# Splitting weights on ScalarE and VectorE instead of GpSimd in a hybrid decoder step

## What is computed

```python
xn = rmsnorm(x, norm1_g)
rg_x, rg_y, q, k, v, g_lr, g_out, m_a, m_b = split(xn @ w_in)
xc = causal_conv4(rg_x);  h = rglru(xc, ...)           # gated linear recurrence over time
ya = (h * gelu(rg_y)) @ w_branch_a
o  = gla(q * dk**-0.5, k, v, log_alpha)                # chunked gated linear attention, state S
yb = (rmsnorm(o) * g * silu(g_out)) @ w_branch_b
x  = x + (sigmoid(m_a) * ya + sigmoid(m_b) * yb) @ w_out
u  = causal_conv3(rmsnorm(x, norm2_g) @ w_ffn_up);  gate, val = split(u)
x  = x + (gelu(gate) * val) @ w_ffn_down
y  = rmsnorm(x, final_norm_g)                          # also all final states
```

## Time and profile before

| | us |
|---|---|
| three timed runs, median | 1968.67 (1965.29 to 1969.84) |
| the profiled execution, device time | 1968.59 |
| its span in the trace | 1966.8 |
| TensorE matmul busy | 1914.4 (97%) |
| VectorE busy | 906.0 (46%) |
| GpSimd busy | 701.9 (36%) |
| ScalarE busy | 420.9 (21%) |

### The profile page before, as it was taken

The page is one execution under the profiler, slowest core; times in us unless marked ns, Lnnn a source line. Parts: engine busy times, 40 slices in busy tenths (PEclk is TensorE's granted clock), DMA queues, the critical chain, the costliest instruction groups (busy, mean ns, idle before and its releaser), DMA issues.

```text
span 1966.8 us, 29051 instructions
## 1 busy us (share of the span) xinstructions
PE 1914.4 (97%) x11890; PEld 1885.9 (96%) x11890; DVE 906.0 (46%) x916; ACT 420.9 (21%) x480; POOL 701.9 (36%) x324
## 2 busy tenths in 40 slices
PE   7999999999999999999999999999999999999997
PEld 6999888888889999999999999999999999999997
DVE  5211277787865311141134555536253535354546
ACT  4000144555532100020011121102010101010115
POOL 3333232232234343344344333333333333334353
PEclk9999998999999999999999999999999999999999
DMA  5221123222212111131113211111111111111112
GB/s 192 87 89 43 44 88 109 89 77 91 77 43 75 43 43 53 43 130 48 48 48 125 65 44 43 44 54 44 44 44 53 43 44 45 53 43 44 53 52 86
DMA packets 48167, 127.11 MB, mean 65 GB/s; under 512 B 6952, under 2 KB 20008, under 8 KB 48080
## 3 DMA queue, kind: packets, MB, share of 16 engines
q1 hardware_dynamic: 27744, 88.39, 13.5%
q10 hardware_dynamic: 20352, 37.64, 5.5%
HBM read 108.14 MB, written 18.14 MB: 64 GB/s over the span
## 4 chain that ended last, share of the span: by engine, by line
PE 92%; DVE 4%; issue 3%; ACT 1%; DMA 0%; DVEq 0%; SPq 0%
PE acc L416 84%; PE acc L594 1%; PE acc L755 1%; PE small L514 1%; PE small L517 1%; DVE rg_xc_h L1327 1%; PE small L526 1%; DVE rg_xc_h L1324 1%; DVE rg_ext L1149 0%; PE small L607 0%; DVE gla_bc_keT L1214 0%; PE small L755 0%; PE small L489 0%; DMA x_in<-in_x 0%; PE small L533 0%
## 5 line engine op out<-in xcount | busy, mean ns | idle before, releaser
L382 POOL TENSOR_TENSOR w_hi<-w_raw,ones 128x1024 fp32r<-128x1024 f32 x149 | 288.3, 1935 | 1215.5 <-PE acc L416 1203.7
L416 PE MATMUL acc<-xn_hi,w_hi 128*128 128x346 f32 (+1 forms) x2520 | 553.8, 328 | 15.9 <-DVE xn_lo L1136 12.1
L416 PE MATMUL acc<-xn_lo,w_hi 128*128 128x346 f32 (+1 forms) x2520 | 541.8, 323 | 0.0
L416 PE MATMUL acc<-xn_hi,w_lo 128*128 128x346 f32 (+1 forms) x2520 | 540.1, 323 | 0.0
L416 PEld LDWEIGHTS acc<-xn_hi,w_hi 128*128 128x128 f32 x2520 | 427.5, 190 | 21.5 <-issue 12.9
L416 PEld LDWEIGHTS acc<-xn_lo,w_hi 128*128 128x128 f32 x2520 | 429.7, 190 | 0.0
L416 PEld LDWEIGHTS acc<-xn_hi,w_lo 128*128 128x128 f32 x2520 | 428.6, 190 | 0.0
L384 POOL TENSOR_TENSOR w_lo<-w_raw,w_hi 128x1024 fp32r<-128x1024 f32 x149 | 384.2, 2578 | 11.7
L1520 DVE TENSOR_TENSOR residual<-acc,residual 128x1032 f32<-128x1032 f32 x56 | 69.0, 1232 | 115.8 <-PE acc L416 115.8
L1491 DVE SCALAR_TENSOR_TENSOR tmp<-val_ext,ffn_params,tmp 128x1024 f32<-128x1024 f32 x48 | 97.9, 2040 | 39.4 <-ACT tmp L1069 36.6
L1491 DVE SCALAR_TENSOR_TENSOR gate_conv<-gate_ext,ffn_params,gate_conv 128x1024 f32<-128x1024 f32 x48 | 92.0, 1917 | 40.6 <-ACT gate_conv L1063 37.7
(11 more groups left out here) (216 smaller groups left out, 2082.6 us busy)
## 6 DMA issues: line engine op xcount, KB each, us to landing
w_raw<-in_w SPq DMA_DIRECT2D x153, 512.0 KB, 3.5
ha_scratch<-rg_gelu_ha ACTq DMA_DIRECT2D x8, 519.0 KB, 3.5
h<-ha_scratch ACTq DMA_DIRECT2D x8, 519.0 KB, 7.0
residual<-in_x ACTq DMA_DIRECT2D x8, 519.0 KB, 7.6
gla_qk_pair<-qk_scratch ACTq DMA_DIRECT2D x8, 512.0 KB, 5.8
smp_v_rows<-smp_v_scratch ACTq DMA_DIRECT2D x8, 512.0 KB, 6.5
out_gla_sample<-smp_state ACTq DMA_DIRECT2D x8, 512.0 KB, 3.8
smp_state<-in_gla_state ACTq DMA_DIRECT2D x7, 512.0 KB, 5.0
```

The costliest lines, as they stand in the source:

```text
L382: nc.gpsimd.tensor_tensor(whi[s], raw[s], one, ALU.mult).then_inc(w_hi_done[s], 1)
L416: mm = nc.tensor.matmul(acc[g][:, n, 0:cw], w[s][:, t * P:(t + 1) * P], x[:, c0 + n * cw:c0 + (n + 1) * cw], start=a, stop=z)
```

## The change

The loop of splits on GpSimd is removed; it keeps the units 1 and 2 and the last three, so 147 of the 153 units move. A new function `w_high` on ScalarE makes the hi part with a Copy, and `w_low` on VectorE subtracts it from the raw weight. Calls of both stand at fixed places of the two streams, one pair for each unit u, behind the eviction of unit u, and split unit u+2.

```diff
             split(0, 1)
-            with pool.Fori(1, (N_UNITS - GRP) // 2) as i:
-                split(i, 0)
-                split(i, 1)
+            split(1, 0)
...
+            def w_high(u, per=0, i=0):
+                s, n = slot_of(u), nth(u, per, i)
+                act.wait_ge(w_loaded[s], 16 * n + 16)
+                act.wait_ge(unit_done[s], n)
+                nc.scalar.activation(whi[s], raw[s], ACT.Copy).then_inc(w_hi_done[s], 1)
...
                 nc.scalar.activation(gy[:, late], gy[:, late], ACT.Gelu_apprx_tanh).then_inc(gelu_ready, 1)
+                w_high(U_RG + 3, 2, j)
                 plain()
                 act.wait_ge(gate_mm, 2 * j + 1)
...
+            def w_low(u, per=0, i=0):
+                s, n = slot_of(u), nth(u, per, i)
+                dve.wait_ge(w_hi_done[s], n + 1)
+                nc.vector.tensor_tensor(wlo[s], raw[s], whi[s].bitcast(F32), ALU.subtract).then_inc(w_split[s], 1)
...
                 nc.vector.tensor_copy(col(rgo, j, RGW, RGW), ext[:, C + 3 - RGW:C + 3]).then_inc(rgo_kept, 1)
+                w_low(U_RG + 2, 2, j)
                 o_copy(n, PAIR, c0, 0, sb6)
...
                 state(n, PAIR, 1, sb7)
+                w_low(U_RG + 3, 2, j)
...
                     evacuate(U_GO + s, 2, i, g, T[s][:, late], cols=LATE)
+                    w_low(U_GO + 2 + s, 2, i)
...
                 nc.vector.tensor_tensor(view3(e_t[:, 2 + L0:2 + L1]), accl[g], view3(rms[:, late]), ALU.mult).then_inc(acc_free[g], 1)
+                w_low(u + 2, per, i)
                 dve.wait_ge(bias_sem, F + 1)
...
                 nc.vector.tensor_tensor(view3(blkd(X2, m)), accd[g], view3(blkd(X2, m)), ALU.add).then_inc(acc_free[g], 1)
+                v = (2, 5, 7).index(m) if m in (2, 5, 7) else GRP
+                if v < n_low:
+                    w_low(u_last - GRP + 3 + v, per, i)
```

More of the change, by code:

```diff
@@ L813, in _ @@
                 for s, g in ((0, 1), (1, 0)):
+                    w_high(U_QKV + s + 2, 2, i)
                     act.wait_ge(acc_free[g], G_QKV[g] + i + 1)
@@ L889, in sample_tokens @@
                 nc.scalar.activation(t, bank[0:NS, :], ACT.Copy).then_inc(sT_ready, 1)
+            w_high(U_QKV + 10)
             ke_tokens(0, NMETA)
@@ L894, in _ @@
             load_qk(PAIR, NMETA)
+            w_high(U_QKV + 11)
+            with act.Fori(1, 4) as i:
+                w_high(U_QKV + 10, 2, i)
+                w_high(U_QKV + 11, 2, i)
             act.wait_ge(acc_free[0], G_RG[0])
@@ L958, in rg_body @@
                     .then_inc(xbias_ready, 1)
+                w_high(U_RG + 2, 2, j)
                 act.wait_ge(sS_ready, j + 1)
@@ L1008, in gate_o @@
                     nc.scalar.activation(T[s][:, late], T[s][:, late], ACT.Silu).then_inc(silu_done, 1)
+                    w_high(U_GO + 2 + s, 2, i)
                     plain()
@@ L1016, in _, with gate_b @@
                 gate_o(i)
-            with act.Fori(0, KB) as j:
+            def gate_b(j):
                 act.wait_ge(acc_free[1], G_B[1] + j + 1)
                 nc.scalar.activation(T[2][:, late], T[2][:, late], ACT.Tanh, scale=0.5).then_inc(tanh_done, 1)
+                w_high(U_B + 2, 2, j)
+            with act.Fori(0, KB - 1) as j:
+                gate_b(j)
+                w_high(U_B + 3, 2, j)
+            gate_b(KB - 1)
             for k in range(KB):
@@ L1027, in _ @@
                 act.dma_start(blkl(HA, k), ha_scr[k][:, late]).then_inc(hl_loaded[k], 16)
+            w_high(U_B + 3, 2, KB - 1)
             for k in range(KB):
@@ L1030, in _, with gate_a @@
                 nc.scalar.activation(blkl(HAH, k), blkl(HA, k), ACT.Copy).then_inc(hah_done, 1)
-            with act.Fori(0, KB) as j:
+            def gate_a(j):
                 act.wait_ge(acc_free[1], G_A[1] + j + 1)
                 nc.scalar.activation(T[2][:, late], T[2][:, late], ACT.Tanh, scale=0.5).then_inc(tanh_done, 1)
+                w_high(U_A + 2, 2, j)
+            with act.Fori(0, KB - 1) as j:
+                gate_a(j)
+                w_high(U_A + 3, 2, j)
+            gate_a(KB - 1)
             act.wait_ge(acc_free[1], G_OUT[1])
@@ L1038, in _ @@
                 if k == KB - 1:
-                    ready(U_OUT - 1)
+                    w_high(U_A + 3, 2, KB - 1)
                     for m in range(KB):
@@ L1045, in _ @@
             for k in range(KB):
+                w_high(U_OUT + k + 2)
                 act.wait_ge(acc_free[1 - k % 2], G_OUT[1 - k % 2] + k // 2 + 1)
@@ L1055, in _, with ffn_block @@
             norm_factor(sum2_mm, lnr2_done, r2_done, LATE)
-            def ffn_block(F, grp):
+            def ffn_block(F, grp, u, per, i):
                 plain()
@@ L1064, in ffn_block @@
                                      bias=fpr[:, bass.ds(3 * UB + F, 1)]).then_inc(gbias_ready, 1)
+                w_high(u + 2, per, i)
                 act.wait_ge(gconv_step, 3 * F + 3)
@@ L1070, in ffn_block @@
                                      bias=fpr[:, bass.ds(3 * UB + FB + F, 1)]).then_inc(vbias_ready, 1)
+                w_high(u + 3, per, i)
                 act.wait_ge(act_done, F + 1)
@@ L1076, in _, with ffn_group, down_high @@
             GU, GD = GRP, KB // 2
-            def ffn_group(F0_, grp, half):
+            NU, ND = 2 * GRP, GRP
+            per = 2 * (NU + ND)
+            def ffn_group(F0_, grp, half, u0, i=0):
                 for f in range(GRP):
-                    ffn_block(F0_ + f, grp + f)
+                    ffn_block(F0_ + f, grp + f, u0 + 2 * f, per, i)
                     ffn_hi(half, f)
+            def down_high(u0, i, n):
+                for v in range(n):
+                    w_high(u0 + NU + v + 2, per, i)
             act.wait_ge(set_f, 4)
-            ffn_group(0, 0, 0)
+            ffn_group(0, 0, 0, U_FFN)
             gper = 2 * (GU + GD)
             with act.Fori(0, NGRP // 2 - 1) as i:
-                ffn_group(2 * GRP * i + GRP, GU + gper * i, 1)
+                ffn_group(2 * GRP * i + GRP, GU + gper * i, 1, U_FFN + NU, i)
+                down_high(U_FFN + NU, i, ND)
                 act.wait_ge(acc_free[0], G_FFN[0] + 2 * GU + GD + gper * i)
-                ffn_group(2 * GRP * i + 2 * GRP, 2 * GU + GD + gper * i, 0)
+                ffn_group(2 * GRP * i + 2 * GRP, 2 * GU + GD + gper * i, 0, U_FFN + 2 * NU + ND, i)
+                down_high(U_FFN + 2 * NU + ND, i, ND)
                 act.wait_ge(acc_free[0], G_FFN[0] + 3 * GU + 2 * GD + gper * i)
             n = NGRP // 2 - 1
-            ffn_group(GRP * (NGRP - 1), GU + gper * n, 1)
+            ffn_group(GRP * (NGRP - 1), GU + gper * n, 1, U_FFN + NU + n * per)
+            down_high(U_FFN + NU + n * per, 0, 1)
             act.preload_act_table_set(LN_EXP)
@@ L1161, in stage_qk @@
                     evacuate(U_QKV + s, 2, i, g, (rt, it)[s])
+                    w_low(U_QKV + s + 2, 2, i)
             stage_qk(0)
@@ L1279, in _ @@
             evacuate(U_QKV + 8, 0, 0, 1, blk(V, 0))
+            w_low(U_QKV + 10)
             scores(0, NMETA)
             evacuate(U_QKV + 9, 0, 0, 0, blk(V, 1))
+            w_low(U_QKV + 11)
             with dve.Fori(1, 4) as i:
                 evacuate(U_QKV + 8, 2, i, 1, blk(V, 2 * i))
+                w_low(U_QKV + 10, 2, i)
                 evacuate(U_QKV + 9, 2, i, 0, blk(V, 2 * i + 1))
+                w_low(U_QKV + 11, 2, i)
             o_copy(0, NMETA, 0, 0, sb7)
@@ L1414, in _ @@
                 evacuate(U_B, 2, j, 1, T[2][:, late], cols=LATE)
+                w_low(U_B + 2, 2, j)
                 dve.wait_ge(tanh_done, j + 1)
@@ L1418, in _ @@
                     .then_inc(acc_free[0], 1)
+                w_low(U_B + 3, 2, j)
             for k in range(KB):
@@ L1430, in merge_gate @@
                 evacuate(U_A, 2, j, 1, T[2][:, late], cols=LATE)
+                w_low(U_A + 2, 2, j)
             def merge(j):
@@ L1509, in ffn_block, with add @@
                 nc.vector.tensor_tensor(blkd(AL, b), act_t[:, down_c], blkd(AH, b).bitcast(F32), ALU.subtract).then_inc(actl_done, 1)
-            def add(n_down, grp, m, u_last, per, i):
+            def add(n_down, grp, m, u_last, per, i, n_low):
                 g = 1 - m % 2
@@ L1524, in _, with ffn_group @@
             per, gper = 2 * (NU + ND), 2 * (GU + GD)
-            def ffn_group(F0_, u0, grp0, half, n_down=None, i=0):
+            def ffn_group(F0_, u0, grp0, half, n_down=None, i=0, n_low=GRP):
                 def down(m):
-                    add(n_down, grp0 + GRP, m, u0 + NU + ND - 1, per, i)
+                    add(n_down, grp0 + GRP, m, u0 + NU + ND - 1, per, i, n_low)
                 for f in range(GRP):
```

4 lines of the change are left out of this document (3 added, 1 removed).

## The result

The changed kernel takes 1937.68 us (median of 4 runs, 1936.29 to 1939.25) against 1968.46 us for the kernel before (4 runs): a ratio of 0.9846, 95% interval 0.9829 to 0.9863. The forecast was 1939 us. The profiled execution takes 1936.35 us, its span 1934.5, which is 32.3 us less than the span before.

The account below looks back on a forecast made before the run. TensorE, busy 97% of the span, bounds the kernel; its waits in the recurrent rounds were the gain. 1968.6 - 35.2 (rounds) + 4.9 (down products) + 0.2 (output gate) = 1938.5, so 1939 us; range 1930 to 1955.

Parts of the forecast that it names:

- The cause: Recurrent rounds: GpSimd's split holds VectorE's 10-column product and sum, so TensorE waits 3.0 us for scores before `O_pair`.
- The hold: Recurrent rounds: time GpSimd's split adds to VectorE's 10-column product and sum, 1.57 + 2.08 = 3.65 us a round.
- The Copy on the path: Recurrent rounds: a weight Copy on ScalarE before the first tanh adds 0.8 us to the path to the scores.
- the wait: Recurrent rounds: TensorE's wait before `O_pair` shrinks from 3.0 to about 0.1 us, and the half clock should go.
- the bound without residue: Recurrent rounds: upper bound on the saving, 5.3 us a round, 37 in all.
- The 0.2 us for `o_copy`: Recurrent rounds: a subtraction ahead of `o_copy` delays the state product that needs it; 0.2 us a round added.
- VectorE's subtraction at the round's end: Recurrent rounds: the added subtraction behind the gelu is covered by VectorE's slack; costed at nothing, at most 1 us a round.
- The down products: FFN groups' last blocks: `add(0)` ends late for TensorE's column block 2, 0.7 us each, 4.9 us for seven.
- The output gate's first unit: Output gate: the split of U_GO + 2 comes 0.2 us late for TensorE, once.
- Short operations that are long by themselves: Rival, recurrent rounds: the 10-column operations are long without GpSimd, nothing is freed; 1982.6 us, chance 0.09.
- Half the hold: Rival, recurrent rounds: only the 10-column product is freed, wait 2.2 us, clock still drops; 1968 us, chance 0.05.
- Leftover wait: Rival, recurrent rounds: added Copy and subtraction run late, 1 to 2 us more a round; 1946 to 1960 us, chance 0.15.

Follow-up runs that it names:

- e2: Kernel before, all splits still on GpSimd, only the split of each recurrent round's first unit waits for `rgo_kept`; 1932.72 us, ratio 0.9823.
- e3: Kernel before, only the second half (`w_lo`) of the split of each round's first unit waits for `rgo_kept`; 1940.73 us, ratio 0.9867.
- e1: Kernel before, only the splits of the recurrent rounds (units 19 to 34) moved to ScalarE and VectorE; 1933.04 us, ratio 0.9827.
- e4: Changed kernel, the split of each recurrent round's first unit back on GpSimd at its old time; 1976.52 us, ratio 1.0034.
- e5: Changed kernel, in each FFN group's last block the value unit's subtraction put behind `add(0)`; 1934.85 us, ratio 0.9834.
- e7: Changed kernel, the splits of the recurrent rounds (units 19 to 34) back on GpSimd; 1972.72 us, ratio 1.0017.
- e6: Changed kernel, the Copy ahead of each recurrent round's first tanh cut into 16 Copies of 64 columns; 1944.71 us, ratio 0.9883.

## Why the prediction was right, step by step

**The cause** was right. The hold was estimated at 3.65 us a round; 4.09 us for the two operations became 0.31, so 3.78 us were freed. e2 and e3 show that it is the overlap in time, and that each half of the split holds the operation beside it. The order in the kernel before becomes plain with one more of its rows, between those of the earlier trace rows:

```profile
417.28 2.31 DVE L1325 TENSOR_TENSOR_SCAN rg_xc_h<-rg_a,rg_i_b 128x1040 f32<-128x1040 f32 x1
```

`w_hi` runs first and the product waits for it; the scan is then ahead of `w_lo` (417.28 against 417.41), which lasts 4.38 us there and 2.38 in e2: it waited for the scan. The sum then waits for `w_lo`. The engines pass one thing to and fro, and VectorE lost its turn twice.

The Trainium skill's page SBUF — State Buffer, section Who interferes with whom, says just this: the two exclude each other for the whole instruction, in order of issue. The traces agree, with 0.14 us and 2.30 us for the same operation in one execution (e1). The Trainium skill's page Perfetto Trace Analysis, section GPSIMD Engine Instruction, calls GpSimd's spans unreliable, which I gave as the word against it; here the ends that match within 0.03 us were real, since moving GpSimd's instruction moved VectorE's end (e2, e3).

**The Copy on the path** was put at 0.8 us and is 0.2; this is the term of the sum that was most off. The gate product of this round, by the timelines of the kernel before and of the changed one:

```profile
394.94 1.93 PE L594 MATMUL acc<-rg_xc_h,rg_gate_weights 128*128 128x350 f32 x6
```

```profile
379.26 1.93 PE L592 MATMUL acc<-rg_xc_h,rg_gate_weights 128*128 128x350 f32 x6
```

The prediction counted from 395.10, where the chain takes this product up, 0.16 us late; its sum is not hurt, as it ends a round on the same kind of row, but before and after must be counted from one kind of start. From the gate product to the scores' end a round took 425.07 - 394.94 = 30.13 us and now takes 405.80 - 379.26 = 26.54, which is 3.59 less, of the 3.78 that were freed: 0.19 is left for the Copy. ScalarE's first tanh does start 0.54 us later (2.60 behind the gate product against 2.06), but at the 10-column product 0.17 is left (20.80 against 20.63). e2, which frees the same without a Copy, ends its scores 26.37 us behind the gate product (408.51 - 382.14), 0.17 less, and e4 agrees with 0.2. I carried a delay at its source to the end of the chain as if nothing on the way had slack.

**So the wait** of 0.1 us became a margin of 0.47, and a round is TensorE's own work alone: 38.05 us, against the 26.96 + 11.03 = 37.99 that the prediction had for it and 38.35 that it forecast. Seven rounds gave 37.28, the bound without residue (37), not 35.2. The 0.2 us for `o_copy` went the same way.

**VectorE's subtraction at the round's end** was costed at nothing, rightly: VectorE still idles 2.64 us ahead of the operation that had 2.72 in the earlier trace rows. What covers its 1.23 us, by the timelines, is the sample state's first operation, L1298, which took 3.24 us beside GpSimd's split in this round and takes 1.14 now; the prediction named it without a number.

**The down products** were put at 0.7 us each, 4.9 in all; the stretch grew by 3.6, 0.5 each: column block 2 starts 8.65 us behind the group's first `act_lo` product where it was 8.15 (1234.60 - 1225.95, 1269.94 - 1261.79). Of this 0.33 is the marked wait (2.3 us in seven); the rest is that block 2 began before the product ahead of it had ended (1269.94 against 1269.42 + 0.64 = 1270.06) and no longer does. The chain was right and its joints too large: the Copy starts at 1228.26, 0.09 before the bias ends, and the subtraction 0.04 behind the Copy (1229.34 against 1229.30), where I had 0.15.

**The output gate's first unit** was put at 0.2 us late; the middle is 0.2 to 0.3 longer in after, e5 and e7 (694.5) than in before, e1 and e2. The place is the one named, as the changed kernel's timeline has it:

```profile
557.71 1.23 DVE L1194 TENSOR_TENSOR w_lo<-w_raw,w_hi 128x1024 fp32r<-128x1024 f32 x1 [3.45 <-ACT w_hi L776]
...
559.07 0.73 PE L414 MATMUL acc<-xn_hi,w_hi 128*128 128x346 f32 x3
```

The unit's first products start 0.13 us behind the subtraction's end and take 0.73 us where they took 0.63 before; against the eighth gate product the next ones are 0.15 us later than before.

**What was not in the sum:** the way to the first gate product, 1.2 us longer in this execution. From 17 to 231 us TensorE is at the same place in both kernels, to 0.1 us; from 232 to 234 us its granted clock is 1.00 before and 0.50 after, and 1.1 of the 1.2 us arise there. The same kernel differs by 2.95 us on this way from one execution to another (below), so these runs don't show that the change causes the 1.2 us. The errors partly cancel: 2.1 more from the rounds and 1.3 less lost at the down products, against 1.2 at the start. That the forecast came within 1.3 us of the median is in part luck.

The three rivals are settled. Short operations that are long by themselves: L1374 starts at 402.37, before the scan ahead of it ends at 402.45, and takes 0.15 us. Half the hold: e3 built its mirror image and both halves count. Leftover wait: e6 shows that it was near, 0.84 us away at the tanh and 0.47 at the scores.

The best versions are e2 and e1, 3.6 and 3.3 us under the changed kernel that ran beside them (1936.32); the FFN column of the table has them 3.7 and 3.9 us lower.

## What to carry to other kernels

An operation that lasts eight to ten times as long as its neighbour of the same width, and ends when another engine's instruction ends, was being held here: look for such a pair before costing the engines. Then ask first whether the other instruction can simply run later; one wait on GpSimd gave here all that moving 147 splits gave, and the moves had a price elsewhere, where VectorE's chain had no margin. And when an operation is added to an engine, follow every one of its successors to TensorE, the release of an accumulator too, not only the chain at hand.

## What the hardware showed that I had not expected

**GpSimd is held as well.** `w_lo` takes 2.38 us clear of VectorE's scan and 4.38 beside it. GpSimd's own durations show the same hold from the other side.

**The clock falls at another moment in another execution of one program.** The changed kernel's runs lie near 1936.2 or near 1939.2 us. Two profiled executions of it, the first of 1936.35 us, the second of 1939.23, each with the row behind a pause of 1.85 us that TensorE has at 219 to 221 us in both, then windows of 2 us:

```profile
221.07 0.60 PE L487 MATMUL small<-ident,gla_kd_ke_vcopy 128*16 128x128 f32 x4 [1.85 <-issue]
...
222.00:224.00 2.00, 1.56 (x13) 0.93 (x12) 0.00 (x0) 1.78 (x4) 0.00 (x0) 1.00 0.44 139
224.00:226.00 2.00, 2.00 (x18) 1.94 (x18) 0.45 (x2) 1.23 (x3) 0.00 (x0) 1.00 0.42 139
...
228.00:230.00 2.00, 1.59 (x6) 1.62 (x7) 0.53 (x4) 0.57 (x2) 0.00 (x0) 0.50 0.03 8
```

```profile
221.21 0.60 PE L487 MATMUL small<-ident,gla_kd_ke_vcopy 128*16 128x128 f32 x4 [1.85 <-issue]
...
222.00:224.00 2.00, 1.76 (x11) 0.89 (x8) 0.00 (x0) 1.37 (x3) 0.00 (x0) 0.60 0.41 129
224.00:226.00 2.00, 2.00 (x10) 1.71 (x9) 0.00 (x0) 0.96 (x3) 0.00 (x0) 0.50 0.43 145
```

After the same pause the second execution is at the 1.2 GHz level from about 223 us on, the first only from about 228 (the column of the granted clock: 1.00, 1.00, 0.50 against 0.60, 0.50). Their first gate products start at 265.10 and 268.05, 2.95 us apart, and the runs differ by 2.88. e2's runs show the same pair of levels (1932.3 and 1935.2). What makes the clock fall early or late there stays open.

**Small joints.** ScalarE starts an independent operation 0.1 us before the one ahead of it ends (1228.26 against 1228.35), and VectorE follows ScalarE's Copy by 0.04 us.
